# Modulation weights loaded by column halves, with the first channel blocks made between the halves

## What is computed

```python
mod = jax.nn.silu(c) @ w_ada[l] + b_ada[l]
shift, scale, gate = jnp.split(mod, 3, axis=-1)
h = rms_norm(x, norm_g[l]) * (1.0 + scale[:, None]) + shift[:, None]
proj = h @ w_in[l]
(qa, ka, va, za, aa, ba, qb, ckv, zb, qi, ki, wi, gl) = jnp.split(proj, pts, axis=-1)
```

## Time and profile before

| | us |
|---|---|
| median of 3 runs | 1423.94 |
| lowest and highest | 1423.18, 1425.76 |
| profiled execution | 1422.03 |
| its span in the trace | 1419.9 |
| PE busy in it | 1375.4 |
| DVE, ACT, POOL busy | 926.2, 716.5, 596.5 |

### The profile page before, as it was taken

How to read it: one execution, slowest core, us unless ns; L and a number is a source line. 1 busy time by engine, 2 the same in 40 slices (tenths; PEclk the granted TensorE clock), 3 DMA queues, 4 the chain that set the end, 5 groups by cost and what they waited for, 6 DMA issues and landing times.

```text
span 1419.9 us, 27055 instructions
## 1 busy us (share of the span) xinstructions
PE 1375.4 (97%) x10296; PEld 840.6 (59%) x10304; DVE 926.2 (65%) x1954; ACT 716.5 (50%) x1521; POOL 596.5 (42%) x717
## 2 busy tenths in 40 slices
PE   7899999999999999999999999999999999999997
PEld 6545994444444466666666666654446888844444
DVE  3869787777343567778878785546715777747344
ACT  4848777785434454555555554332114777701111
POOL 0083677778761532531531530003114777764000
PEclk9999999999999999999999999999999999999999
DMA  9410333333323322222222222437563101085132
GB/s 372 130 38 2 104 100 114 115 114 120 104 83 123 91 62 61 77 80 57 77 62 68 84 77 63 125 96 260 174 238 104 32 17 31 17 292 163 37 101 89
DMA packets 137641, 147.49 MB, mean 104 GB/s; under 512 B 16706, under 2 KB 109738, under 8 KB 135852
## 3 DMA queue, kind: packets, MB, share of 16 engines
q1 hardware_dynamic: 136668, 141.31, 31.6%
q10 hardware_dynamic: 720, 4.46, 0.8%
q0 software_dynamic: 128, 0.03, 0.0%
HBM read 114.40 MB, written 31.15 MB: 103 GB/s over the span
## 4 chain that ended last, share of the span: by engine, by line
PE 53%; DVE 6%; DMA 3%; issue 2%; ACT 2%; POOL 2%; SPq 1%; DVEq 0%; POOLq 0%; ACTq 0%
PE ps L94 14%; PE ps L96 14%; PE ps L95 13%; DVE g_yq L1569 2%; PE ps L2379 2%; DMA merge_half<-g_shared 1%; DVE g_o L1703 1%; POOL g_shared L1334 1%; PE ps L1948 1%; PE ps L1845 1%; POOL g_shared L1336 1%; PE ps L1969 1%; PE ps L1953 1%; PE ps L1952 1%; PE ps L1968 1%
## 5 line engine op out<-in xcount | busy, mean ns | idle before, releaser
L94 PE MATMUL ps<-g_h_hi,g_piece_hi 128*128 128x512 f16 x544 | 206.9, 380 | 1.6 <-PEq L2590 1.6
L95 PE MATMUL ps<-g_h_lo,g_piece_hi 128*128 128x512 f16 x544 | 206.3, 379 | 0.0
L96 PE MATMUL ps<-g_h_hi,g_piece_lo 128*128 128x512 f16 x544 | 206.2, 379 | 0.0
L1334 POOL TENSOR_TENSOR g_shared<-g_shared 128x120 f32<-128x120 f32 (+14 forms) x120 | 56.1, 467 | 193.7 <-DMA g_shared<-diagonal_blocks 183.1
L946 DVE TENSOR_SCALAR_CACHE_REDUCE a_ada<-a_ada,a_s_all 128x896 bf16<-128x896 f32 (+1 forms) x124 | 113.1, 968 | 1.0
L94 PE MATMUL ps<-g_o,g_h_hi 128*128 128x128 f16 (+2 forms) x424 | 101.4, 266 | 1.7 <-DVE l_b L2500 1.6
L96 PE MATMUL ps<-g_o,g_h_lo 128*128 128x128 f16 (+2 forms) x424 | 101.4, 266 | 0.4
L95 PE MATMUL ps<-g_o,g_h_hi 128*128 128x128 f16 (+2 forms) x416 | 98.3, 264 | 0.0
L1569 DVE SCALAR_TENSOR_TENSOR g_yq<-e_raw,g_taps,g_yq 128x1024 f32<-128x1024 f32 x60 | 87.7, 1461 | 7.6 <-ACT g_yq L1398 5.8
L96 PEld LDWEIGHTS ps<-g_h_hi,g_piece_lo 128*128 128x128 bf16 x544 | 53.3, 98 | 64.4 <-issue 0.3
L94 PEld LDWEIGHTS ps<-g_h_hi,g_piece_hi 128*128 128x128 f16 x544 | 53.3, 98 | 54.3 <-issue 2.2
(11 more groups left out here) (431 smaller groups left out, 4055.6 us busy)
## 6 DMA issues: line engine op xcount, KB each, us to landing
a_w<-in_w_in SPq DMA_DIRECT2D x17, 1024.0 KB, 5.5
g_piece<-in_w_in SPq DMA_DIRECT2D x34, 512.0 KB, 4.0
channel_gates<-a_ada SPq DMA_DIRECT2D x48, 256.0 KB, 2.2
g_shared<-diagonal_blocks SPq DMA_DIRECT2D x32, 256.0 KB
a_ada<-in_w_ada ACTq DMA_DIRECT2D x4, 1024.0 KB, 9.4
a_x<-in_x SPq DMA_DIRECT2D x8, 512.0 KB, 9.2
delta_gate<-a_ada SPq DMA_DIRECT2D x16, 256.0 KB, 2.5
g_shared<-sums_by_head SPq DMA_DIRECT2D x8, 512.0 KB, 4.0
```

The costliest lines, as they stand in the source:

```text
L94: pe.matmul(out, a_hi, b_hi, start=first, stop=False)
L95: pe.matmul(out, a_hi, b_lo, start=False, stop=False)
L96: return pe.matmul(out, a_lo, b_hi, start=False, stop=last)
L1334: nc.gpsimd.tensor_tensor(part, table[:, j, :, j + 1:BASE], tc[:, :, j:j + 1].broadcast_to([P, NT, left]), ALU.mult).then_inc(sub, 1)
```

## The change

Every weight block is loaded as two column halves: half 0 holds the columns of channel blocks 0 to 3 of shift and scale, half 1 those of 4 to 7, each 128 x 2 x 512 numbers (512 KB) in pieces of 2 KB. The first halves of all eight blocks and tokens 0 to 3 are asked for first, then the second halves. ACT asks for weights 0 to 3 in both halves and for tokens 1 and 3, SP for the rest. The block k = 3 is put into the place of the later query weights `w32[:, 1]`, so their load (L223 before) now waits for `total(1)` (`mod_mm` = 2).

PE and DVE work through the first halves, then `total(0)` and `modulation(0)`; channel blocks 0 to 3 and the first queries are made before and between the work on the second halves, then follow `total(1)`, `modulation(1)` and blocks 4 to 7. PE turns blocks 0 to 3 ahead of its last first half. The three unread products are gone. The rounding `high_q(1)` stands behind all eight `raised` instead of behind the sixth.

```diff
+            tokens_in(sp, 0)
+            sp.dma_start(g.const[:, 0:P], g.const_dram[:, 0:P]).then_inc(id_in, 16)
+            tokens_in(sp, 2)
+            for k in (4, 5, 6, 7):
+                weights_in(sp, 0, k)
+            sp.dma_start(w32[:, 0, :, 0:P], win[:, :, C_QI:C_QI + P]).then_inc(q_in[0], 16)
+            for k in (4, 5, 6, 7):
+                weights_in(sp, 1, k)
             for i in range(4, NT):
...
+            sp.wait_ge(mod_mm, 2)
             sp.dma_start(w32[:, 1], win[:, :, C_QI + UNIT:C_QI + 2 * UNIT]).then_inc(q_in[2], 16)
...
-            for n in range(3):
-                nc.tensor.matmul(bank(n), ada[:, 0, 0:P], ada[:, 0, 0:BANK], start=True, stop=True)
...
+            def weigh(m, part):
+                k = by_pe[m]
+                pe.wait_ge(ada_in[part][k], 16)
+                for n in range(2):
+                    for j in range(4 * part, 4 * part + 4):
+                        nc.tensor.matmul(sums_at(n, j), ada_of(k)[:, n * D + j * P:n * D + (j + 1) * P], g.sc_col[:, k:k + 1].broadcast_to([P, P]),
+                                         start=(m == 0 and j % 4 == 0), stop=False, skip_group_check=True)
...
             pe.wait_ge(silu, 1)
+            for m in range(3):
+                weigh(m, 0)
+            for n in range(4):
+                turn(n)
+            weigh(3, 0)
             total(0)
+            weigh(0, 1)
+            weigh(1, 1)
+            pe.wait_ge(q_half, 1)
+            first_query(0)
+            first_query(1)
+            turn(4)
+            weigh(2, 1)
+            first_query(2)
+            first_query(3)
+            weigh(3, 1)
+            for n in (5, 6, 7):
                 turn(n)
+            total(1)
+            pe.wait_ge(q_ready, 1)
+            for k in range(4, KD):
+                last = first_query(k)
...
             for k in range(4):
-                act.dma_start(ada[:, k, :], g.w_ada[0, k * P:(k + 1) * P, 0:2 * D]).then_inc(ada_in[k], 16)
+                weights_in(act, 0, k)
+                if k < 2:
+                    tokens_in(act, 2 * k + 1)
+            for k in range(4):
+                weights_in(act, 1, k)
             act.wait_ge(col_ok, 1)
```

## The result

| | before | after |
|---|---|---|
| median, same chip | 1424.83 (9 executions) | 1430.21 (9 executions) |
| lowest and highest | 1421.47, 1431.79 | 1425.51, 1431.69 |
| profiled execution | 1422.03 | 1431.69 |
| its span | 1419.9 | 1429.5 |

After / before is 1.0033, 95% interval 1.0016 to 1.0049: about 5 us slower, where +9.2 was forecast. The time lies inside the range given. That the profiled execution of after stands 9.7 above that of before looks like a full hit, but both are single executions, this one of after the slowest of its nine.

The account below looks back on a forecast made before the run. PE, busy 97%, was taken to bound the kernel, its later chain starting from ACT's square of token 4. 44.2 (`total(1)`) + 2.55 + 4.94 = 51.7 against 42.52: +9.2; 1423.94 + 9.2 = 1433.1, range 1427.0 to 1436.0.

Parts of the forecast that it names:

- the mark: Square of token 4 on ACT, 42.52 before and forecast at 51.7; its shift of +9.2 was carried to the end.
- The loss of clock: PE behind some 7 us idle, ahead of `total(0)`: starts at the slow pace of 1.2 GHz, 1.7 us lost.
- Both coverings: Second halves land by about 32, late `w32[:, 1]` by 51 (needed at 56.5): both claimed hidden, holding up nothing.
- The stall: ACT's ten DMA issues fill its queue; the tenth ends at 12.0, so silu comes at 13.3 instead of 8.36; 0.65.
- The count of about 75 waiting pieces: DMA queue: an issue ends when all pieces ahead of it fit into about 75 (69 to 99).
- PE runs through: Rival: PE has no gap from silu to `total(1)` if token 3 is scaled by 19.5; 4.5 gained, 1419.4; chance 0.07.
- No stall: Rival: ACT's issues stay short, silu stays at 8.36; mark at 45.0 to 46.7, +2.5 to +4.2, 1427.5; chance 0.20.
- The second loss of clock: Rival: PE's turns of the second token half also run at the slow pace, 1.7 more, 1434.8; chance 0.08.

Follow-up runs that it names:

- the kernel with ten transfers: Kernel before in its own order of work, but ACT issues weights 0 to 3 in halves and tokens 1 and 3; median 1435.39, ratio 1.0074.
- the run with eight: Changed kernel, but SP instead of ACT asks for tokens 1 and 3, leaving ACT eight transfers; median 1431.20, ratio 1.0038.
- the run with the copies: Kernel before with a chain of eight unread copies on ACT ahead of the square of token 4; median 1438.76, ratio 1.0114.

## Why the prediction was right or wrong

**The front: right in its steps.** Forecast and the trace of after: issues of ACT end 12.0, 12.05; silu 13.3, 13.38; token 3 scaled 27.0, 26.56 (2.84 a token, not 2.96); `total(0)` 32.25, 32.73; `raised(0)` 34.8, 35.17; `total(1)` 44.2, 44.77; the mark 51.7, 52.25. So +9.2 forecast, +9.2 to +9.7 measured in three traces. Two terms were off and nearly cancel. The loss of clock was charged with 1.7 and cost 2.6: 1.7 on the turns and 0.9 on the half behind them (from 26.56 to `total(0)` at 32.73 are 6.17, where the forecast has 5.25); token 3 came 0.4 earlier than forecast. PE's idle time ahead of them, forecast 7, is 5.18. Both coverings held: second halves and the late query weights (issued at 46.86) hold up nothing.

**The stall: right, and less of a cause than I made it.** That ACT's tenth issue waits was the decisive choice, and the row shows 6.02 us. By the sentence of the Trainium skill (DMA: Bandwidth & Descriptors, section "Issuing engines are not separate DMA queues") that issue time is usually small, this would have been 1427.5; the tenth issue of 6.02 us, and of 8.72 in the kernel with ten transfers, disagree with it here, while the eight issues done by 5.12 agree. The count of about 75 waiting pieces fits the end of the tenth issue: in the trace of after ACT's queue had moved 946 packets by 12.05, 59 of its pieces on each engine (forecast 62), so 78 of the 137 ahead still waited, and 70 in the kernel with ten transfers. It does not fit which issue is the first to wait: the eighth issue of the run with eight ended with 88 waiting (119 less 31), the ninth of after with 90 (120 less 30), and neither was held. One fixed size of the queue doesn't explain both, and what starts the stall stays open. That 12.0 came so close to 12.05 is in part luck: 4.3 MB were to have moved by then and 3.50 had, 1.17 of them on SP's queue and not 1.9. And the stall covered the next limit. Without it (SP issues all halves) the mark gains 2.5 to 3.0, where the forecast and its rival lie 5.0 to 6.7 apart, for DVE's order then makes tokens 1 to 3 wait for weights 4. Of the +9.2, the stall is 2.5 to 3.0, the turns ahead of the totals with the last first half behind them 2.1, DVE's order 3.8 (1.2 of it behind the start of `total(0)`, which then kept the full pace) and 0.6 to 0.8 remain, each by one trace of the run that took it away. The amounts depend on the order of taking away: with DVE's order left, the stall's removal by moving tokens to SP gained nothing.

**The end: the step that failed.** "What the change adds to it or takes from it, I carry to the end of the kernel" holds to 980 us, up to falls of the clock, and fails at 1021 to 1034: there the changed kernel gets 3.5 us back. The waits that I read ended at 140 us; behind them, at 1028 us, stand 1.57 us at L2019, which could fall away, among some 19 us of waits in all. The list could not have shown that it does. The rest is noise of the base: 1423.94 was the median of three, 97 executions have 1425.4 as their mean, so the same +9.2 gives 1434.6 by the better base and the miss is 5 us rather than 3.

**The rivals.** "PE runs through" failed at its own condition. The scaling of token 3 came at 21.58 at the best, not by 19.5, and the mark was then 43.36. "No stall" had the wrong sum (45.0 to 46.7 at the mark, 49.24 measured). The second loss of clock happened in after too (0.64 in the mean of 50 to 58 us), but ended before the turns began; only in the run with the copies did they pay for it.

Slower by over 0.2% was given 0.90; 1.0033 and the pooled +4.3 (0.30%) lie only just above that bound, closer than the forecast had it. The range held the time by the room it had below, and that room was there for another reason (a short stall) than the one that came.

## What to carry to other kernels

A DMA issue is an instruction of an in-order stream: count what is queued ahead of it, and put the first compute of that engine ahead of the issues that can wait. When one limit is priced, ask which wait lies under it; here the stall, a token step behind a `weigh`, and turns ahead of a total each covered the next, and removing the first alone gave back less than a third. A shift at the front has to be followed through every later wait of the bounding engine, and a difference of five microseconds in 1425 needs repeated traces of both kernels, because one execution of the same code differs from the next by as much.

## What the hardware showed beyond that

Smaller pieces went with a lower rate. In pieces of 2 KB the same engines moved less per second than in pieces of 8 KB with all 16 busy; no run changed the size alone. DMA totals of before at 12 to 15 us, and of after at 14 to 20 us:

```profile
DMA packets 217, 1.29 MB, mean 430 GB/s; under 512 B 22, under 2 KB 62, under 8 KB 62
```

```profile
DMA packets 1208, 2.33 MB, mean 388 GB/s; under 512 B 70, under 2 KB 70, under 8 KB 1208
```

The two queues do not share bytes evenly when their pieces differ. In the kernel with ten transfers, ACT's halves (2 KB pieces) stood beside SP's whole blocks (8 KB): from 12 to 15 us the queues moved 138 and 139 pieces, but 0.26 MB on ACT's and 1.01 MB on SP's, and ACT's tenth issue grew from 6.02 to 8.72 us. Equal numbers of pieces are what service in turn would give.

The granted clock reads 1.00 at PE's first work in a trace although its pace is half there: 16 rows in the first 3.38 us of the earlier trace rows, and in after 32 rows in 6.01 us from 13.64, where 16 take 1.95 later. Both stretches lie ahead of the first change of the clock that their trace records (11.95 and 18.22); there, go by the pace of rows. At the later slow stretches, as at 26.61, the column and the pace agree.
